# Transposing the keys once and copying them to the other partitions, and moving three steps in the order of a hybrid attention, Hyena and MoE layer

## The chip, the cores and the metric

One core of one Trainium2 chip runs the whole kernel. The metric is the device time of one execution in microseconds (us); of several executions the median is taken. The engines are TensorE (PE, with its weight loads as PEld), VectorE (DVE), ScalarE (ACT), GpSimd (POOL) and SyncE (SP), which here only issues DMAs.

## The reference

The layer serves 1024 latent tokens and 128 context tokens with the same weights. The part that the change touches, cut down:

```python
h = x * (1 + sc1) + sh1                       # modulation columns, from SiLU(cond) @ w_mod
proj = h @ w_in                               # "in-projection": q, k, v and three Hyena parts
q, k = rope_2d(rms_norm(q)), rope_2d(rms_norm(k))
k_all = concatenate([k, cached context keys]) # 2 kv heads of 64, 8 query heads
s = einsum(q, k_all) * scale ; p = softmax(s) ; o = p @ v_all

z = position_features(t)                      # Hyena's filters
h = sin(freq * (z @ w1 + b1))                 # first sine layer
h = sin(freq * (h @ w2 + b2))                 # second sine layer
h = (h @ w3) * exp(-t * |decay|)              # the taps, in a window
g = two_sided(h) ; g = g * rsqrt(sum(g * g))  # norm of each channel
spec = rfft(g)                                # spectra of the filters
```

After that come two gated long convolutions by Fourier transforms, the output projection, a layer norm, a router, 33 blocks of experts and a last layer norm.

## The kernel before

Each engine has its own list of instructions, written out by hand and run in that order. Engines wait for each other on named counting semaphores (`pe.wait_ge(sem("skip_scaled"), n)`). So what stands behind a waiting instruction on the same engine waits too.

**Front.** PE multiplies the conditioning vectors with eight 1 MB chunks of `w_mod`: `modulation_parts(c)` is the product (16 records on L1139), ACT's `copy_parts(c)` brings it to SBUF, and `modulation_columns(c)` sums it into columns. Chunks come by DMA on SP's queue in order; chunks 4 to 7 are issued when an earlier product is done. Between them stand `hidden(0)` and `hidden(1)`, the two products of the sine layers. DVE turns each product into an argument (L1853 to L1858) and ACT takes the sine (L846).

**Four passes.** The filters are made in four passes of 256 channels. In pass p, `taps(p, j)` on PE makes nine tiles of taps, DVE weighs them (`weigh_taps`), ACT squares them (L863), and POOL adds the squares (L650, L654, L648). `norms(p)` on PE sums these over partitions (four products with one column); DVE makes scales of them (`norm_scales`) and releases `skip_scaled`; `skip_rows(p)` on PE turns the scales into rows, which DVE adds to the first row of taps (L1626 on 1x512 elements) before it releases `taps_skipped`. DVE also makes the tiles of the transform, in three parts that release `tiles_transformed`. `spectrum(p, i)` on PE makes 22 products per pass, each copied by ACT (L871) and stored by a DMA. In between stand the 27 tiles of the in-projection, `project_qkv(m)`: eight products of 128x256 each, copied by ACT (L879). Tiles 0 to 2 are in pass 0's first part, and pass p starts with tile `first` = 5, 12 or 19. The first tiles need the modulated input, which ACT makes in `modulate` (L903, eight instructions for the first 512 tokens). The last five spectra of a pass are left over into the next one (`SPEC_LEFT`).

**Keys.** Before attention, keys and queries are split into a high and a low part (`split_keys`, `high_heads`, `low_heads` on DVE), turned by PE, and copied from PSUM by ACT. The contraction of a score runs over 128 partitions: a query's high part in 0 to 63 and its low part in 64 to 127, against a key part that stands in both halves. `KEY_BLOCKS` are four blocks (2 kv heads, high and low) of ten tiles of 128 keys. `turn_keys(n)` makes both halves by two ordinary products with the identity per tile (L1374, `tile_position` 0 and 64), and ACT copies 128x1280 (L995). Then `scores(0)` starts the attention loop of 72 steps (9 query tiles, 8 heads), in which DVE takes the maximum (L2056), ACT the exponent (L1004), and PE turns the probabilities (L1113) and multiplies them with the values (L1443).

Of the kernel before, what the change touches and what calls it, by code (L numbers as in the profile page):

```python
# [22 lines left out]
F32 = mybir.dt.float32  # L23
# [133 lines left out]
def build(nc, I, O):  # L157
    ctx = ExitStack()
    with ctx:
# [17 lines left out]
        def sem(name):  # L177
            if name not in sems:
                sems[name] = ctx.enter_context(nc.semaphore(name))
            return sems[name]  # L180
# [638 lines left out]
        def _(act):  # L819
# [172 lines left out]

            for n, (v, s) in enumerate(KEY_BLOCKS):
                act.wait_ge(sem("rows_turned"), n + 1 + (n > 1))
                act.copy(kT[:, s, v, :], PS[:, 1536 * (n % 2):1536 * (n % 2) + 10 * P]).then_inc(sem("rows_copied"), 1)  # L995
                if n == 1:
                    act.wait_ge(sem("rows_turned"), 3)
                    act.copy(qT[:, :, 0:P], PS[:, 3072:4096].rearrange("p (h t) -> p h t", h=HEADS)).then_inc(sem("rows_copied"), 1)
# [109 lines left out]
        def _(pe):  # L1108
# [17 lines left out]
            def modulation_parts(c):  # L1126
                if c < COND_CHUNKS:
                    pe.wait_ge(sem(f"cond_w_loaded{c % 4}"), 16 * (c // 4 + 1))
                else:
                    pe.wait_ge(sem("late_w_loaded"), 16 * (c - COND_CHUNKS + 1))  # L1130
                if c > COND_CHUNKS:
                    pe.wait_ge(sem("mod_copied"), c - COND_CHUNKS)
                if c:
                    pe.wait_ge(sem("parts_copied"), c)
                at = 512 * parts_bank(c)
                for half in range(2):
                    for j in range(4):
                        k = 2 * j + half
                        last = nc.tensor.matmul(PS[32 * j:32 * j + 32, at:at + CHUNK], cond_wide[:, k, :], mod_weights(c)[:, k, :],  # L1139
                                                start=half == 0, stop=half == 1, tile_position=(0, 32 * j))  # L1140
                last.then_inc(sem("parts_product"), 1)

            def modulation_columns(c):
                pe.wait_ge(sem("parts_copied"), c + 1)
                for i in range(2):
                    last = mm(bank(7, 2, at=2 * (2 * c + i)), parts(c)[:, P * i:P * (i + 1)], part_sum)
                last.then_inc(sem("cols_product"), 1)
# [29 lines left out]
            def skip_rows(p):  # L1177
                pe.wait_ge(sem("skip_scaled"), p + 1)
                for lc in range(2):
                    for b in range(2):  # L1180
                        last = mm(bank(4 + lc, P, rows=1, at=HALF + P * b), col_s[:, 2 * b + lc:2 * b + lc + 1], ident)
                last.then_inc(sem("skip_row"), 1)
# [37 lines left out]
            modulation_parts(0)  # L1220
            modulation_parts(1)
            modulation_columns(0)
            modulation_parts(2)
            modulation_columns(1)
            hidden(1)
            for c in range(3, 6):
                modulation_parts(c)
                modulation_columns(c - 1)
# [15 lines left out]
            for p in range(PASSES):  # L1244
                first, end = QKV_BY_PASS[p:p + 2]
                if p:
                    project_qkv(first)
                    for i in range(SPEC_LEFT, N_SPEC):
                        spectrum(p - 1, i)
                    norms(p)  # L1250
                    project_qkv(first + 1)
                    project_qkv(first + 2)
                    skip_rows(p)
                    project_qkv(first + 3)
                    project_qkv(first + 4)
                else:
                    norms(0)
                    skip_rows(0)
                    for m in range(3):
                        project_qkv(m)  # L1260
                for i in range(SPEC_CTX):
                    spectrum(p, i)
                for m in range(first + (5 if p else 3), end):
                    project_qkv(m)
                for i in range(SPEC_CTX, SPEC_ODD):
                    spectrum(p, i)
                for i in range(SPEC_ODD, SPEC_LEFT):
                    spectrum(p, i)
                if p + 1 == PASSES:
                    for i in range(SPEC_LEFT, N_SPEC):  # L1270
                        spectrum(p, i)
                    continue
                for j in range(NTILE):
                    taps(p + 1, j)
# [90 lines left out]
            def turn_keys(n):  # L1365
                v, s = KEY_BLOCKS[n]
                pe.wait_ge(sem("rows_split"), n + 1 + (n > 1))
                if n >= 2:
                    pe.wait_ge(sem("rows_copied"), n - 1)
                for t in range(NTILE + 1):  # L1370
                    key = {NLAT: 9, NTILE: 8}.get(t, t)
                    at = 1536 * (n % 2) + P * key
                    for u in range(2):
                        last = nc.tensor.matmul(PS[HD * u:HD * (u + 1), at:at + P], k_split[:, s, t, HD * v:HD * (v + 1)].bitcast(F32),  # L1374
                                                ident, start=True, stop=True, tile_position=(0, HD * u))
                last.then_inc(sem("rows_turned"), 1)

            def turn_head(out, h):
# [19 lines left out]
            def scores(i):  # L1398
                h, t = ATT[i]
                v = h // GQA  # L1400
                pieces = ((0, 512), (512, 1024), (1024, 1152)) if t < NLAT else ((1152, 1280),)
                if i:
                    pe.wait_ge(sem("max_ready"), i)
                if t and h == 0:
                    pe.wait_ge(sem("heads_copied"), 4 * t)
                for s in range(2):
                    for a, (k0, k1) in enumerate(pieces):
                        last = mm(bank(a, k1 - k0), qT[:, h, P * t:P * (t + 1)], kT[:, s, v, k0:k1], s == 0, s == 1)
                last.then_inc(sem("scores_ready"), 1)

            def turn_probs(i):
                n = NTILE if ATT[i][1] < NLAT else 1
                if i:
                    pe.wait_ge(sem("probsT_d"), i)
                if i - 1 in HEADS_AT:
                    pe.wait_ge(sem("heads_copied"), 4 * HEADS_AT[i - 1][0] + HEADS_AT[i - 1][1] // 2 - 3)
                if i in HEADS_AT:
                    turn_heads(i)
                pe.wait_ge(sem("exp_ready"), i + 1)
                if i:  # L1420
                    pe.wait_ge(sem("probsT_a"), i)
                for k in range(n):
                    last = turn(PS[:, 1536 + P * k:1536 + P * (k + 1)], probs[:, i % 2, P * k:P * (k + 1)])
                last.then_inc(sem("probs_transposed"), 1)
# [37 lines left out]
                last.then_inc(sem("scales_spread"), 1)  # L1462

            pe.wait_ge(sem("rows_copied"), len(KEY_BLOCKS) + 1)
            scores(0)
            for i in range(len(ATT)):
                if i + 1 < len(ATT):
# [140 lines left out]
        def _(dve):  # L1608
# [434 lines left out]
                tt(q_split[:, :, 1, :], q, q_split[:, :, 0, :].bitcast(F32), ALU.subtract).then_inc(sem("rows_split"), 1)  # L2043

            dve.wait_ge(sem("cache_loaded"), 32)
            split_keys(0)
            high_heads(0)
            low_heads(0)
            split_keys(1)

            def maximum(i):
                n = NTILE * P if ATT[i][1] < NLAT else P
# [12 lines left out]
            for i in range(len(ATT)):  # L2065
                if i + 1 < len(ATT):
                    maximum(i + 1)
                dve.wait_ge(sem("probs_transposed"), i + 1)
                if i >= 4:
                    dve.wait_ge(sem("attn_product"), i // 2 - 1)  # L2070
                if ATT[i][1] < NLAT:
                    dve.tensor_copy(probsT[:, i % 4, 4:9, :], PS[:, 2048:2688].rearrange("p (t n) -> p t n", t=5)).then_inc(  # L2072
                        sem("probsT_d"), 1)
                else:
                    give(dve.tensor_copy(bn[:, 0:1], ones[:, 0:1]), "probsT_d")
                if i in HEADS_AT:
                    t, h = HEADS_AT[i]
                    dve.tensor_copy(qT[:, h:h + 2, P * t:P * (t + 1)],
                                    bank(5, 2 * P, at=P).rearrange("p (h t) -> p h t", h=2)).then_inc(sem("heads_copied"), 1)
                h, t = ATT[i]  # L2080
                if t + 1 < NTILE and h == 0:
                    dve.wait_ge(sem("rows_turned"), 5 + t if t else 3)
                    high_heads(t + 1)
                    low_heads(t + 1)
                if i in SCALE_AT:
                    scale_attention(SCALE_AT[i])
# [264 lines left out]
```

## Time and profile before

| | |
|---|---|
| median of 3 runs | 1656.86 us (1655.42 to 1658.33) |
| the profiled execution's own time | 1657.55 us |
| its span in the trace | 1655.7 us |
| PE busy | 1501.1 us (91%) |
| DVE, ACT, POOL busy | 947.7, 362.8, 367.4 us |
| filters and in-projection | 0 to 300 us, PE busy 253.9 |
| keys turned, first scores | 726.3 to 740.4 us |

Times in the rows count from the span's start. A row of a timeline gives start, length, engine, line, operation and count, and in brackets how long the engine sat idle before it and who released it. A product of f32 operands leaves two records, a transpose one. The share of busy time says little here, since PE is busy nearly everywhere: a change can only act where PE sits idle, or runs at its lower clock, or is given less work.

### The profile page before, as it was taken

To read this page: it belongs to the slowest core of one execution; us is meant where nothing else is said; L and a number is where in the kernel's file an instruction comes from. 1 tells how busy PE (TensorE), PEld (TensorE's weight loads), DVE (VectorE), ACT (ScalarE), POOL (GpSimd) and SP (SyncE) were. 2 spreads that over 40 slices of the span, in tenths; PEclk is the share of its full clock that TensorE was granted. 3 is DMA by queue.
4 is the path that set the end of the run, shared out by engine and by line. 5 is a ranking of instruction groups with operands and counts; after the bars stand their busy time and mean duration, and the time that the engine had idled before them with its cause. 6 is when DMAs were issued, how large, how long until landed. Compare 5 with 4: busy or idle time off the path is not lost. (4 is left out here: it accounts for less than half of the span.)

```text
span 1655.7 us, 22893 instructions
## 1 busy us (share of the span) xinstructions
PE 1501.1 (91%) x8630; PEld 1086.7 (66%) x8630; DVE 947.7 (57%) x1577; ACT 362.8 (22%) x696; POOL 367.4 (22%) x623
## 2 busy tenths in 40 slices
PE   7689988999998899949999997999489999999985
PEld 3467766444444688848888874455378888888852
DVE  3867876366654999966666653443733333333326
ACT  2553342111110111115655551010000000000004
POOL 0330330011110000000311317746222212222114
PEclk9799998999999999979999997999589999999998
DMA  9422123233321212230000004211458898998845
GB/s 320 148 69 83 44 75 118 67 104 122 122 90 67 90 58 64 70 109 1 2 2 1 2 1 155 74 64 51 165 202 319 338 331 321 332 338 327 306 171 218
DMA packets 102743, 229.27 MB, mean 138 GB/s; under 512 B 12807, under 2 KB 70759, under 8 KB 93896
## 3 DMA queue, kind: packets, MB, share of 16 engines
q1 hardware_dynamic: 78968, 195.86, 33.1%
q0 software_dynamic: 10736, 19.77, 3.4%
q10 hardware_dynamic: 12960, 12.59, 2.3%
q8 instruction: 50, 0.82, 0.2%
q14 instruction: 29, 0.24, 0.0%
HBM read 204.66 MB, written 38.98 MB: 147 GB/s over the span
## 5 line engine op out<-in xcount | busy, mean ns | idle before, releaser
L1110 PE MATMUL PS<-buffer 128*128 128x128 f32 (+7 forms) x5638 | 1255.5, 380 | 90.6 <-DVE buffer L1626 28.1
L1110 PEld LDWEIGHTS PS<-buffer 128*128 128x128 f32 (+2 forms) x5638 | 870.6, 195 | 448.0 <-issue 314.1
L1626 DVE TENSOR_TENSOR buffer<-buffer 128x512 f32<-128x512 f32 (+16 forms) x446 | 258.5, 604 | 26.8 <-ACT buffer L965 11.8
L1626 DVE TENSOR_TENSOR buffer<-PS,buffer 128x512 f32<-128x512 f32 (+2 forms) x143 | 94.4, 690 | 129.6 <-PE PS L1110 116.2
L1113 PE MATMUL PS<-buffer 128*128 128x128 f32 x1136 | 157.0, 280 | 12.7 <-DMA buffer<-moe_inputs,buffer 5.5
L1113 PEld LDWEIGHTS PS<-buffer 128*128 128x128 f32 x1136 | 130.2, 153 | 39.9 <-issue 29.0
L1626 DVE TENSOR_TENSOR buffer<-buffer,PS 128x256 f32<-128x256 f32 (+3 forms) x55 | 27.6, 502 | 205.7 <-PE PS L1110 195.1
L2056 DVE TENSOR_SCALAR_CACHE_REDUCE buffer<-PS 128x1152 f32<-128x1152 f32 (+1 forms) x72 | 89.1, 1238 | 36.4 <-PE PS L1110 35.6
L1004 ACT ACTIVATE buffer<-buffer 128x1152 f32<-128x1152 f32 (+1 forms) x72 | 83.8, 1164 | 107.6 <-DVE buffer L2056 107.5
L1080 ACT ACTIVATE buffer<-PS 128x256 f32<-128x256 f32 x33 | 12.6, 383 | 367.1 <-PE PS L1110 367.1
L2072 DVE COPY buffer<-PS 128x640 f32<-128x640 f32 x64 | 52.8, 825 | 63.1 <-PE PS L1113 62.3
L1443 PE MATMUL PS<-buffer 128*64 128x128 f32 x1168 | 79.3, 279 | 6.1 <-ACT buffer L1037 4.7
L1443 PEld LDWEIGHTS PS<-buffer 128*64 128x64 f32 x1168 | 62.6, 137 | 19.7 <-ACT buffer L1037 13.8
L678 POOL TENSOR_TENSOR buffer<-buffer 128x256 f32<-128x256 f32 (+4 forms) x45 | 17.9, 399 | 258.1 <-ACT buffer L1010 254.7
L1966 DVE TENSOR_SCALAR buffer<-PS,buffer 128x1024 f32<-128x1024 f32 (+1 forms) x24 | 21.0, 877 | 93.8 <-PE PS L1110 93.4
L2257 DVE SCALAR_TENSOR_TENSOR buffer<-PS,buffer 128x1024 f32<-128x1024 f32 x33 | 42.4, 1284 | 40.5 <-PE PS L1110 40.5
L662 POOL TENSOR_TENSOR buffer<-buffer 2x256 f32<-2x256 f32 x16 | 11.9, 746 | 235.4 <-ACT buffer L841 235.4
L1639 DVE SCALAR_TENSOR_TENSOR buffer<-buffer 128x512 f32<-128x512 f32 (+6 forms) x69 | 56.6, 820 | 2.4
L770 POOL COPY buffer<-buffer 128x1 int32 x32 | 5.8, 183 | 232.4 <-DVE buffer L2257 232.4
L2241 DVE COPY buffer<-PS 128x1024 f32<-128x1024 f32 x33 | 40.4, 1225 | 17.6 <-PE PS L1113 17.6
L648 POOL TENSOR_TENSOR buffer<-buffer 128x256 f32<-128x256 f32 x8 | 8.7, 1085 | 168.2 <-ACT buffer L863 168.2
L761 POOL DMA_INDIRECT expert_outputs<-buffer x34 | 34.4, 1012 | 47.1 <-POOL buffer L770 25.5
(170 smaller groups left out, 966.2 us busy)
## 6 DMA issues: line engine op xcount, KB each, us to landing
buffer<-in_exp_w_gate SPq DMA_DIRECT2D x33, 1024.0 KB, 6.8
buffer<-in_exp_w_up SPq DMA_DIRECT2D x33, 1024.0 KB, 9.2
buffer<-in_exp_w_down SPq DMA_DIRECT2D x33, 1024.0 KB, 9.0
buffer<-in_w_mod SPq DMA_DIRECT2D x24, 1024.0 KB, 7.0
filter_spectra<-buffer ACTq DMA_DIRECT2D x88, 128.0 KB, 1.7
buffer<-filter_spectra SPq DMA_DIRECT2D x44, 256.0 KB, 2.6
buffer<-in_w_in SPq DMA_DIRECT2D x9, 1024.0 KB, 5.2
buffer<-expert_outputs SPq DMA_DIRECT2D x4, 1536.0 KB, 17.1
```

Of the source, the lines that this page charges most:

```text
L761: pool.indirect_dma_start(out=y_d[:, :], out_offset=bass.IndirectOffsetOnAxis(ap=rows, axis=0), in_=ybuf[:, s, :], in_offset=None, bounds_ ...
L1004: act.activation(probs[:, i % 2, 0:n], probs[:, i % 2, 0:n], ACT.Exp, bias=nmax[:, i:i + 1], scale=-1.0, accum_out=psums[:, i:i + 1]).then ...
L1110: return nc.tensor.matmul(out, lhsT, rhs, start=start, stop=stop)
L1113: return nc.tensor.transpose(out, in_, ident)
L1443: last = nc.tensor.matmul(PS[HD * u:HD * (u + 1), at:at + P], vals, probsT[:, (first + u) % 4, a, :], start=a == 0, stop=a == len(tiles) - ...
L1626: return dve.tensor_tensor(out, a, b, op)
L1639: own(dve.scalar_tensor_tensor(out, a, s, b, ALU.mult, op))
L1966: own(dve.tensor_scalar(out[:, t0:t1], PS[:, ps0 + t0:ps0 + t1], w[1], w[3], ALU.mult, ALU.add))
L2056: dve.tensor_scalar(probs[:, i % 2, 0:n], PS[:, 0:n], -1.0, None, ALU.mult, ALU.min, accum_out=nmax[:, i:i + 1]).then_inc(sem("max_ready"), 1)
L2072: dve.tensor_copy(probsT[:, i % 4, 4:9, :], PS[:, 2048:2688].rearrange("p (t n) -> p t n", t=5)).then_inc(sem("probsT_d"), 1)
L2241: dve.tensor_copy(xgT[:, s, :, :], PS[:, 0:1024].rearrange("p (k n) -> p k n", k=KT)).then_inc(sem("xT_ready"), 1)
L2257: dve.scalar_tensor_tensor(ybuf[:, s, :], PS[:, 2048:3072], row_scale[:, s, 0:1], row_gain, ALU.mult, ALU.mult).then_inc(sem("y_ready_to_s ...
```

## The change

Three edits.

1. `turn_keys` makes one transpose per tile, into partitions 0 to 63. ACT copies 64x1280 instead of 128x1280. A new step on DVE, `double_keys(n)`, copies each block from partitions 0 to 63 to 64 to 127, ahead of the first maximum. PE waits for it before `scores(0)`. The semaphore of the query copies is merged with that of the key copies; their waits count four higher.
2. `hidden(1)` stands before `modulation_parts(2)` instead of behind `modulation_columns(1)`.
3. In pass 0, in-projection tiles 0 and 1 stand between `norms(0)` and `skip_rows(0)`. In passes 1 to 3 one tile moves ahead of `norms(p)`, and the others close up.

```diff
@@ ACT
-                act.copy(kT[:, s, v, :], PS[:, 1536 * (n % 2):1536 * (n % 2) + 10 * P]).then_inc(sem("rows_copied"), 1)
+                act.copy(kT[0:HD, s, v, :], PS[0:HD, 1536 * (n % 2):1536 * (n % 2) + 10 * P]).then_inc(sem("rows_copied"), 1)
@@ PE
             modulation_columns(0)
+            hidden(1)
             modulation_parts(2)
             modulation_columns(1)
-            hidden(1)
@@ PE
+                    project_qkv(first + 1)
                     norms(p)
-                    project_qkv(first + 1)
                     project_qkv(first + 2)
+                    project_qkv(first + 3)
                     skip_rows(p)
-                    project_qkv(first + 3)
                     project_qkv(first + 4)
                 else:
                     norms(0)
+                    project_qkv(0)
+                    project_qkv(1)
                     skip_rows(0)
-                    for m in range(3):
-                        project_qkv(m)
+                    project_qkv(2)
@@ PE
-                    for u in range(2):
-                        last = nc.tensor.matmul(PS[HD * u:HD * (u + 1), at:at + P], k_split[:, s, t, HD * v:HD * (v + 1)].bitcast(F32),
-                                                ident, start=True, stop=True, tile_position=(0, HD * u))
+                    last = turn(PS[0:HD, at:at + P], k_split[:, s, t, HD * v:HD * (v + 1)].bitcast(F32))
@@ PE
             pe.wait_ge(sem("rows_copied"), len(KEY_BLOCKS) + 1)
+            pe.wait_ge(sem("scores_side_copied"), len(KEY_BLOCKS))
             scores(0)
@@ DVE
+            def double_keys(n):
+                v, s = KEY_BLOCKS[n]
+                dve.wait_ge(sem("rows_copied"), n + 1 + (n > 1))
+                dve.tensor_copy(kT[HD:P, s, v, :], kT[0:HD, s, v, :].bitcast(F32)).then_inc(sem("scores_side_copied"), 1)
+
             split_keys(0)
             high_heads(0)
             low_heads(0)
             split_keys(1)
+            for n in range(len(KEY_BLOCKS)):
+                double_keys(n)
```

PE's list in passes 0 and 1 of the kernel before, from the last taps of pass 0 on. `128x1 x4` is `norms`, `1x128 x4` is `skip_rows`, `128x512` are taps, and `128x256` are in-projection tiles (eight each) and spectra.

```order
L1110 MATMUL PS<-buffer 128x512 x4
L1110 MATMUL PS<-buffer 128x1 x4
L1110 MATMUL PS<-buffer 1x128 x4
L1110 MATMUL PS<-buffer 128x256 x66
L1110 MATMUL PS<-buffer 128x512 x9
L1110 MATMUL PS<-buffer 128x256 x18
L1110 MATMUL PS<-buffer 128x1 x4
L1110 MATMUL PS<-buffer 128x256 x16
```

The same place with the change.

```order
L1110 MATMUL PS<-buffer 128x512 x4
L1110 MATMUL PS<-buffer 128x1 x4
L1110 MATMUL PS<-buffer 128x256 x16
L1110 MATMUL PS<-buffer 1x128 x4
L1110 MATMUL PS<-buffer 128x256 x50
L1110 MATMUL PS<-buffer 128x512 x9
L1110 MATMUL PS<-buffer 128x256 x26
L1110 MATMUL PS<-buffer 128x1 x4
L1110 MATMUL PS<-buffer 128x256 x16
```

In pass 0 two tiles (16 products) moved from behind the skip rows to ahead of them; in pass 1 one tile moved ahead of the norms (26 products there instead of 18).

PE's list from the last products of the convolutions to the first scores, before. `L1374` are the keys, `L1113` the eight query heads.

```order
L1110 MATMUL PS<-buffer 128x256 x352
L1374 MATMUL PS<-buffer 64x128 x40
L1113 MATMUL PS<-buffer 128x128 x8
L1374 MATMUL PS<-buffer 64x128 x40
L1110 MATMUL PS<-buffer 128x512 x2
```

The same place with the change.

```order
L1110 MATMUL PS<-buffer 128x256 x352
L1113 MATMUL PS<-buffer 64x128 x20
L1113 MATMUL PS<-buffer 128x128 x8
L1113 MATMUL PS<-buffer 64x128 x20
L1110 MATMUL PS<-buffer 128x512 x2
```

The number of instructions for the keys is halved, and they are transposes now.

DVE's list from the last split of the keys to the first maxima, as a piece of the difference.

```order
 L1626 TENSOR_TENSOR buffer<-buffer 128x9x64
 L1626 TENSOR_TENSOR buffer<-buffer 128x64
-L2056 TENSOR_SCALAR buffer<-PS 128x1152 x2
-L2072 COPY buffer<-PS 128x640
+L2049 CAST buffer<-buffer 64x1280 x4
+L2063 TENSOR_SCALAR buffer<-PS 128x1152 x2
+L2079 COPY buffer<-PS 128x640
```

Four copies of 64x1280 are new, ahead of the maxima, whose lines are only renumbered.

## Rows read from the trace of the kernel before

**Rows 1.** The page, busy time of PE: us, share, instructions.

```profile
PE 1501.1 (91%) x8630; PEld 1086.7 (66%) x8630; DVE 947.7 (57%) x1577; ACT 362.8 (22%) x696; POOL 367.4 (22%) x623
```

**Rows 2.** Timeline of PE, 5 to 82 us.

```profile
18.95 1.94 PE L1139 MATMUL PS<-buffer 128*32 128x256 f32 x16 [3.04 <-DMA buffer<-in_w_mod]
20.81 5.04 PE L1110 MATMUL PS<-buffer 128*128 128x2 f32 x10
...
41.76 1.07 PE L1139 MATMUL PS<-buffer 128*32 128x256 f32 x16
...
65.20 14.56 PE L1110 MATMUL PS<-buffer 128*1 128x128 f32 x60 [5.44 <-DVE buffer L1626]
81.12 1.26 PE L1110 MATMUL PS<-buffer 128*128 128x256 f32 x3 [1.36 <-ACT buffer L871]
```

**Rows 3.** Timeline of ACT, 0 to 75 us.

```profile
16.67 1.16 ACT L846 ACTIVATE buffer<-buffer 64x1152 f32<-64x1152 f32 x1 [1.27 <-DVE buffer L1858]
...
54.98 0.63 ACT L863 ACTIVATE buffer<-buffer 128x512 f32<-128x512 f32 x1 [3.76 <-POOL buffer L654]
55.51 5.74 ACT L903 ACTIVATE buffer<-buffer 128x512 f32<-128x512 f32 x8
72.02 0.37 ACT L879 COPY buffer<-PS 128x256 f32<-128x256 f32 x1 [10.77 <-PE PS L1110]
```

**Rows 4.** Timeline of DVE, 0 to 75 us.

```profile
25.97 1.47 DVE L1853 TENSOR_SCALAR buffer<-PS,buffer 64x1152 f32<-64x1152 f32 x1 [9.33 <-PE PS L1110]
...
31.81 0.75 DVE L1858 TENSOR_SCALAR buffer<-buffer 64x1152 f32<-64x1152 f32 x1
...
64.78 0.36 DVE L1626 TENSOR_TENSOR buffer<-buffer 128x4 f32<-128x4 f32 x2
```

**Rows 5.** Timeline of SP's queue: the issue of chunk 7 of `w_mod`.

```profile
27.78 0.55 SPq L468 DMA_DIRECT2D buffer<-in_w_mod  x1
```

**Rows 6.** DMA issues, 27.5 to 28.4 us: count, KB, us to landing.

```profile
buffer<-in_w_mod SPq DMA_DIRECT2D x1, 1024.0 KB, 13.4
```

**Rows 7.** Windows: us, busy of PE, PEld, DVE, ACT, POOL, granted clock, DMA.

```profile
65.20:69.60 4.40, 4.40 (x14) 3.01 (x15) 4.20 (x7) 0.00 (x0) 0.00 (x0) 0.50 0.01 4
...
704.50:707.88 3.38, 1.68 (x6) 0.96 (x6) 3.38 (x9) 0.59 (x1) 0.00 (x0) 1.00 0.00 0
...
726.27:731.70 5.43, 5.43 (x52) 5.43 (x54) 3.26 (x8) 0.85 (x1) 0.00 (x0) 0.50 0.90 253
...
738.60:742.00 3.40, 1.83 (x16) 1.20 (x12) 0.21 (x1) 1.23 (x1) 0.00 (x0) 1.00 0.23 95
742.00:749.00 7.00, 4.95 (x30) 3.88 (x30) 5.50 (x9) 3.17 (x5) 0.00 (x0) 1.00 0.01 4
```

**Rows 8.** Timeline of DVE, pass 1.

```profile
124.96 0.16 DVE L1886 TENSOR_SCALAR buffer<-PS 128x4 f32<-128x4 f32 x1 [0.72 <-PE PS L1110]
...
134.66 1.39 DVE L1626 TENSOR_TENSOR buffer<-buffer,PS 1x512 f32<-1x512 f32 x2
```

**Rows 9.** Timeline of ACT, pass 1, and the last copy of keys.

```profile
139.97 0.37 ACT L879 COPY buffer<-PS 128x256 f32<-128x256 f32 x1 [3.08 <-PE PS L1110]
140.40 0.37 ACT L871 COPY buffer<-PS 128x256 f32<-128x256 f32 x1
...
739.12 1.23 ACT L995 CAST buffer<-PS 128x1280 fp32r<-128x1280 f32 x1 [0.96 <-PE PS L1374]
```

**Rows 10.** Timeline of PE, 700 to 760 us.

```profile
726.27 7.26 PE L1374 MATMUL PS<-buffer 128*64 128x128 f32 x80 [16.85 <-DVEq L2033]
...
740.39 1.36 PE L1110 MATMUL PS<-buffer 128*128 128x512 f32 x6 [1.32 <-ACT buffer L995]
743.21 1.37 PE L1110 MATMUL PS<-buffer 128*128 128x512 f32 x6 [1.46 <-DVE buffer L2056]
744.60 1.20 PE L1113 MATMUL PS<-buffer 128*128 128x128 f32 x9
...
752.21 1.42 PE L1113 MATMUL PS<-buffer 128*128 128x128 f32 x11
```

More of the change, by code:

```diff
@@ L1404, in scores @@
                 if t and h == 0:
-                    pe.wait_ge(sem("heads_copied"), 4 * t)
+                    pe.wait_ge(sem("scores_side_copied"), 4 * t + 4)
                 for s in range(2):
@@ L1415, in turn_probs @@
                 if i - 1 in HEADS_AT:
-                    pe.wait_ge(sem("heads_copied"), 4 * HEADS_AT[i - 1][0] + HEADS_AT[i - 1][1] // 2 - 3)
+                    pe.wait_ge(sem("scores_side_copied"), 4 * HEADS_AT[i - 1][0] + HEADS_AT[i - 1][1] // 2 + 1)
                 if i in HEADS_AT:
@@ L2078, in _ @@
                     dve.tensor_copy(qT[:, h:h + 2, P * t:P * (t + 1)],
-                                    bank(5, 2 * P, at=P).rearrange("p (h t) -> p h t", h=2)).then_inc(sem("heads_copied"), 1)
+                                    bank(5, 2 * P, at=P).rearrange("p (h t) -> p h t", h=2)).then_inc(sem("scores_side_copied"), 1)
                 h, t = ATT[i]
```

## The prediction

> **What bounds the kernel now.** I read the page first: PE is busy for 1501.1 us, 91% of the span [rows 1], so a change can gain only where PE idles, runs at its lower clock, or loses work. The timeline of PE then shows the idle places that the edits touch. PE stands still for 5.44 us ahead of 65.20, where DVE releases the skip rows [rows 2]. ACT had the first half of the modulated input ready at 55.51 + 5.74 = 61.25 [rows 3], so tiles 0 and 1 of the in-projection could have run from there. At the keys PE starts at 726.27, and the first scores start at 740.39 [rows 10], 14.12 us later. Last I read the granted clock by windows: it was 1.2 GHz from 65.20 to 69.60 and from 726.27 to 731.70 [rows 7], so both places begin at half speed.
>
> **Edit 2, the second sine layer first.** `hidden(1)` needs the first sine, done at 16.67 + 1.16 = 17.83 [rows 3]. PE was idle until 18.95, waiting for chunk 2; the product is most of the 5.04 us at 20.81 (I take 4.0 of them; the rest are four records of columns) [rows 2]. So it runs 17.9 to 21.9, `modulation_parts(2)` slips by 3.0 us to 21.9, and from chunk 3 on PE is 0.9 us ahead, having filled that much of its idle time. DVE starts its argument at 22.0 instead of 25.97 [rows 4]. This earliness meets a load: chunk 7 is issued at 27.78 and takes 13.4 us to land [rows 5, 6], so 41.18, and its product ran at 41.76 [rows 2]. In the code `modulation_parts(7)` stands ahead of taps 4 to 8, and `copy_parts(7)` ahead of ACT's third square; nothing behind them can come more than 0.55 us sooner. The issue of chunk 6 waits for the product that slips, but 13.4 us to landing is a queue with many microseconds of other loads in it, so a slip of 3 us is covered; if it were not, up to 2 us would be lost. Behind the third square stands POOL's chain of sums, which releases ACT's last one at 54.98 [rows 3], and behind that `modulate`. Edit 2: **0.5 us**, between -1 and 1.
>
> **Edit 3, pass 0.** Tile 0 then starts at 61.25 - 0.5 = 60.75, where PE's work started at 65.20: the same work, from a start 4.45 us earlier (edit 2's 0.5 is in it). The clock rose 4.4 us after PE restarted here, and 5.4 us after at the keys [rows 7]; with 5.4, one more microsecond at half speed costs 0.5. The skip rows fall behind tile 1, about 71 instead of 67. DVE needs them at 71.91 - 0.5 for the row sums; until 65.14 it makes the scales [rows 4], and then tiles of the transform. The two meet within some tenths. The wait of 1.36 us at 81.12, for ACT to copy a spectrum behind the second half of `modulate` [rows 2], moves along with tile 2. So edits 2 and 3 bring 4.45 - 0.5, about **4.0 us**, by the first tap of pass 1; bounds 2.4 and 5.6, for a low stretch that is 3 us longer or shorter, at half speed.
>
> **Edit 3, passes 1 to 3.** Norms come one tile later, and tiles follow each other in 0.37 + 3.08 = 3.45 us [rows 9]. DVE waited 0.72 us for them in pass 1 [rows 8], so it is 3.45 us late there; for passes 2 and 3 I take the same as a bound. Who waits for DVE? `taps_skipped` came at 134.66 + 1.39 = 136.05 [rows 8] and comes at 139.5. The first spectrum behind it ran right behind the tile that ACT copied at 139.97, and was itself copied at 140.40 [rows 9], so with 0.6 us from start to copy it started near 139.8. That leaves 0.3 us: hidden, barely. PE has no idle time to fill ahead of these norms, so nothing is gained either: **0**, three times.
>
 The copy on DVE is new: 0.75 us for 64x1152 from SBUF [rows 4] scales to 0.83 for 1280; the bound above is the rate from PSUM, 1.47 for 1152 [rows 4], so 1.63. The first three hide behind copies of ACT; only the fourth shows. Scores start 10.85 us after PE's start, for 14.12: **3.3 us** earlier (2.0 to 4.4, by DVE's copy and the rise of the clock).
>
> **What it may give back.** PE now does less just ahead of the loop: from the last turn at 8.4 it idles for 2.4 us, does `scores(0)` (1.36), and idles 1.46 for the first maximum, as before [rows 10]. From 704.50 to 707.88 PE worked 1.68 us, and the clock was low after it; from 738.60 to 742.00 it worked 1.83 us and the clock stayed [rows 7]. In the changed kernel the like stretch holds about 1.4 us of work. So I expect the clock to fall to 1.2 GHz around the second scores, and to rise when PE is dense again. Some 6 us at half speed (5.4 at the keys [rows 7]) cost 3.0, less what PE's short waits absorb: **2.6 us** lost, bounds 1 and 4.
>
> **A rule that speaks against edit 1.** From 742 to 749 us a third of PE's work is transposes (1.20 us per step beside 1.4 of scores [rows 10]), PE works 4.95 of 7 us, and the clock stays up [rows 7]: here they seem to count as work, which gives the 3.3. The Trainium skill (TensorE: Matmul & The Clock Gate, Part 4: PE-mode transpose) says that a transpose does not count as PE-busy in the same way. By that rule the rise would not come during the turns, which is rival B.
>
> **The sum.** 4.0 + 3.3 - 2.6 = 4.7 us. From the profiled execution's own 1657.55 that is 1652.85; this execution stands 0.7 above the median of the runs, and I take the sum from the median, 1656.86: **1652.2 us**.
>
> **Rivals.** A measurement of this kernel tells about 0.2%, 3.3 us, from no change.
> - *Forecast, 45%*: 1652.2, its own range 1650 to 1654.5.
> - *A, the clock does not fall in the loop's start, 27%*: 4.0 + 3.3 = 7.3, so 1649.6. For it: at 738.6 it held with little work. Against it: PE will do less still.
> - *B, the clock does not rise on transposes, 8%*: all 48 turns at 0.22 us are 10.6, scores start at 12.9 and gain 1.2 only. The loop then runs at half speed until products alone keep PE dense, an estimated 20 us, 10 lost: 10 - 4.0 - 1.2 = 4.8 slower, 1661.7. For it there is no row in which the clock rose on transposes; against it, 742 to 749.
> - *C, the late norms reach PE, 7%*. DVE is 3.45 us late in each of passes 1 to 3. With 0.3 us of room it is hidden; without any it is 10.35 us, 1656.86 - 4.7 + 10.35 = 1662.5, slower. It decides from about 1.6 us of lateness per pass. For it: 0.3 us is little. Against it: between the norms and `taps_skipped` DVE waits for nothing but the skip rows, and PE's tiles in between are the same number as before.
> - *D, the start in pass 0 is not used, 13%*: the change doesn't do there what it says, because ACT is late or the clock stays low longer; 1 us instead of 4.0, so 1655.2.
>
> **How the numbers follow.** Range 1647.0 to 1657.5: down to A with a clock that falls less often elsewhere, up past D and a weak C; B, most of C and a little below A lie outside. *Faster by over 0.2%* (below 1653.6): 0.38 of the forecast's 0.45, all of A, a little of D, 0.67. *Slower* (above 1660.2): most of B and C, 0.11. *Same*: 0.22.
>
> **What the next profile would show.** Right: DVE's second L1853 near 22.0; tile 0 near 60.7 and its copy by ACT near 67 instead of 72.02; the wait at 81.12 near 77; the first norm scale of pass 1 behind some 4 us of idle DVE, and no wait of PE for DVE at the spectra; the first scores 10.5 to 11.5 us after the first turn; new DVE copies of 0.8 us; a stretch at 1.2 GHz early in the loop. Wrong: PE waiting for DVE in passes 1 to 3, DVE copies above 1.2 us, a low clock through all turns, tile 0 not before 63. What would spoil the number with every step right is the clock: it was low in other stretches too, and each microsecond more or less of that is half a microsecond of time.

## The result and the profile after

The changed kernel takes 1647.17 us, the median of 5 runs (1644.95 to 1649.25); before, on the same chip, it was 1656.86 (1655.01 to 1658.33). The ratio is 0.994, with a 95% interval of 0.9924 to 0.9956: 9.9 us faster by the ratio, 9.7 by the medians, where 4.7 was forecast. On two more chips the same kernel stood at 0.9936 (0.9915 to 0.9958) and 0.9950 (0.9932 to 0.9969). The time lies in the stated range, and the larger chance (0.67, faster by over 0.2%) was on what came; the sum was half of the gain. The profiled execution took 1644.95 for 1657.55, 12.6 us less, so this pair of profiles shows more than the medians do. All ratios compare ordinary executions alone; only e5 below had two others among its 12 (2587 and 7635 us).

First the page of the changed kernel, busy time (answers to [rows 1]). PE has 120 instructions fewer and is busy 6.2 us less, half of what was gained; the rest was idle time.

```profile
PE 1494.9 (91%) x8510; PEld 1080.9 (66%) x8510; DVE 954.3 (58%) x1581; ACT 362.6 (22%) x696; POOL 368.6 (22%) x623
```

The timeline of PE, 15 to 90 us (answers to [rows 2]): start, length, engine, line, number of records, and in brackets the idle time ahead and who ended it.

```profile
17.97 4.10 PE L1110 MATMUL PS<-buffer 64*64 64x512 f32 x6 [0.60 <-ACT buffer L846]
...
41.60 1.07 PE L1139 MATMUL PS<-buffer 128*32 128x256 f32 x16 [1.46 <-DMA buffer<-in_w_mod]
...
58.86 15.94 PE L1110 MATMUL PS<-buffer 128*128 128x1 f32 x68 [8.88 <-POOL buffer L648]
76.16 14.00 PE L1110 MATMUL PS<-buffer 128*128 128x256 f32 x62 [1.36 <-ACT buffer L871]
```

`hidden(1)` stands at 17.97, PE then meets chunk 7 of `w_mod`, and the 5.44 us of idle time behind the norms are gone: the eight records of the norms and 60 more run in one piece. The timeline of ACT, 52 to 80 us, answers to [rows 3]:

```profile
53.81 0.63 ACT L863 ACTIVATE buffer<-buffer 128x512 f32<-128x512 f32 x1 [2.25 <-POOL buffer L654]
54.35 5.74 ACT L903 ACTIVATE buffer<-buffer 128x512 f32<-128x512 f32 x8
65.91 0.37 ACT L879 COPY buffer<-PS 128x256 f32<-128x256 f32 x1 [5.82 <-PE PS L1110]
```

`modulate` starts 1.16 us earlier (54.35 for 55.51), and tile 0 is copied 6.11 earlier, since the skip rows no longer stand ahead of it. By the wait of 1.36, at 76.16 for 81.12, 4.96 us are left. In this profile tile 0 stood behind the norms and not behind `modulate`, which was done at 60.09; in ten of the twelve profiles with the pass 0 edit PE waits 1.64 us for `modulate` there, as the forecast had it. The clock was low for 3.2 us of tile 0, where it was low for 4.4 behind PE's restart before (windows of the changed kernel, columns as in [rows 7]):

```profile
60.56:63.80 3.24, 3.24 (x9) 2.61 (x10) 2.93 (x10) 0.00 (x0) 0.00 (x0) 0.50 0.03 8
63.80:67.00 3.20, 3.20 (x16) 2.81 (x15) 2.89 (x10) 1.09 (x3) 0.00 (x0) 1.00 0.00 0
```

In pass 1 the profile gains 2.9 more, and that is the clock's. The windows of before and then of the changed kernel from 116 to 124 us:

```profile
116.00:124.00 8.00, 5.64 (x15) 4.60 (x15) 6.49 (x5) 2.43 (x7) 3.77 (x4) 0.59 0.19 66
```

```profile
116.00:124.00 8.00, 8.00 (x43) 7.15 (x42) 6.16 (x18) 0.75 (x2) 0.00 (x0) 1.00 0.12 41
```

Pass 2 gave 1.4 of it back. Of all profiled executions, 7 of the 11 with both the sine and the pass 0 edit lack this low stretch, and 2 of the 9 without both: scatter for a good part, and no step of the prediction.

The keys, on the timeline of PE (answers to [rows 10]), on that of DVE, and by windows:

```profile
717.44 7.92 PE L1113 MATMUL PS<-buffer 128*64 128x128 f32 x48 [16.60 <-DVEq L2033]
727.64 1.33 PE L1110 MATMUL PS<-buffer 128*128 128x512 f32 x6 [2.29 <-DVE buffer L2049]
730.43 2.40 PE L1110 MATMUL PS<-buffer 128*128 128x512 f32 x6 [1.46 <-DVE buffer L2063]
732.62 2.12 PE L1113 MATMUL PS<-buffer 128*128 128x128 f32 x9
734.40 2.20 PE L1110 MATMUL PS<-buffer 128*128 128x512 f32 x6
736.43 1.15 PE L1113 MATMUL PS<-buffer 128*128 128x128 f32 x9
```

```profile
725.55 0.82 DVE L2049 CAST buffer<-buffer 64x1280 fp32r<-64x1280 f32 x1 [1.55 <-ACT buffer L995]
726.67 0.82 DVE L2049 CAST buffer<-buffer 64x1280 fp32r<-64x1280 f32 x1 [0.30 <-ACT buffer L995]
```

```profile
717.44:722.60 5.16, 5.16 (x25) 4.49 (x26) 4.08 (x9) 1.89 (x2) 0.00 (x0) 0.50 0.84 251
722.60:729.40 6.80, 4.08 (x31) 3.46 (x29) 2.86 (x4) 3.90 (x4) 0.00 (x0) 1.00 1.02 406
729.40:736.20 6.80, 5.77 (x20) 5.10 (x21) 3.72 (x7) 3.17 (x5) 0.00 (x0) 0.50 0.16 65
982.00:1002.50 20.50, 12.09 (x66) 8.61 (x66) 3.72 (x16) 5.23 (x19) 14.04 (x42) 0.50 0.76 292
```

From the first turn to the first scores it is 10.20 us for 14.12. The clock rose at 722.6, while PE had done nothing but turns since 717.44, and fell again at 729.4: the second scores took 2.40 us for 1.37. Behind the loop (last row) the clock was low for 20.5 us; before, for 23.9:

```profile
994.60:1018.50 23.90, 14.62 (x66) 9.90 (x67) 7.83 (x20) 4.61 (x14) 18.21 (x42) 0.50 0.74 265
```

Comparing start times of the same instruction in the two traces, the 12.6 us of this pair come so: edit 2, 1.2; pass 0, 3.8; clock in passes 1 and 2, 1.5; the end of pass 3, 2.6; turns and copies of the keys, 3.9; low clock early in the loop, -1.7; low clock behind the loop, 2.8. That is 14.1; small losses between (0.3 ahead of the keys, 0.5 in the loop, 0.7 behind it) make it 12.6. Three of these places the prediction did not have: the clock in passes 1 and 2, the end of pass 3, and the clock behind the loop.

One pair of profiles holds much scatter. The experiments below left 18 more, and the averages over the profiles with an edit, less those without it, come nearer to the 9.9 of the runs: start of `modulate` 1.5 (edit 2), from there to the wait of 1.36 3.6 (pass 0), end of pass 3 1.4, keys 3.9, the low clock early in the loop with what comes back behind it -0.6. The sum is 9.8.

### The profile page after: what moved, and what is told of

Same layout as the page of the kernel before. It is cut to its first block, busy times and chain, and to the rows that moved or that the text cites. A ratio compares the mean times of both kernels' runs of the same rounds, so it can differ in the third digit from the quotient of the medians.

```text
span 1643.1 us, 22658 instructions
## 1 busy us (share of the span) xinstructions
PE 1494.9 (91%) x8510; PEld 1080.9 (66%) x8510; DVE 954.3 (58%) x1581; ACT 362.6 (22%) x696; POOL 368.6 (22%) x623
## 4 chain that ended last, share of the span: by engine, by line
PE 76%; DVE 8%; DMA 5%; POOL 4%; issue 4%; ACT 2%; SPq 0%; ACTq 0%; DVEq 0%; POOLq 0%
PE PS L1110 63%; PE PS L1113 7%; PE PS L1442 4%; DVE buffer L1626 3%; DMA buffer<-in_w_mod 3%; PE PS L1139 2%; POOL buffer L654 1%; POOL buffer L650 1%; DVE buffer L1728 1%; DMA buffer<-expert_outputs 1%; DVE buffer L2063 1%; PE PS L1459 1%; ACT buffer L871 1%; DMA filter_spectra<-buffer 0%; ACT buffer L1037 0%
## 5 line engine op out<-in xcount | busy, mean ns | idle before, releaser
L1110 PE MATMUL PS<-buffer 128*128 128x128 f32 (+6 forms) x5638 | 1253.9, 380 | 85.1 <-DVE buffer L1626 22.7
L1113 PE MATMUL PS<-buffer 128*128 128x128 f32 (+1 forms) x1176 | 164.3, 284 | 29.2 <-DVEq L2033 16.6
L1113 PEld LDWEIGHTS PS<-buffer 128*128 128x128 f32 (+1 forms) x1176 | 136.9, 154 | 57.4 <-issue 28.2
L1626 DVE TENSOR_TENSOR buffer<-buffer,PS 128x256 f32<-128x256 f32 (+3 forms) x55 | 27.5, 501 | 206.6 <-PE PS L1110 196.0
L1442 PEld LDWEIGHTS PS<-buffer 128*64 128x64 f32 x1168 | 62.7, 137 | 19.4 <-ACT buffer L1037 13.6
```

The lines of the kernel that those rows point to most:

```text
L1110: return nc.tensor.matmul(out, lhsT, rhs, start=start, stop=stop)
L1113: return nc.tensor.transpose(out, in_, ident)
L1626: return dve.tensor_tensor(out, a, b, op)
```

## The experiments

### Each edit alone

E1 is the change's edit of the keys alone, e2 the sine layer, e3 the order in pass 0, e4 the order in passes 1 to 3, each the diff's own lines put into the kernel before.

> Edit 1 alone on the kernel before: one transpose per key tile, ACT's copy of 64 partitions, DVE's copy to the other 64. Theory M (each edit is worth what its own place shows): first scores 10.2 us after the first turn instead of 14.1, then a stretch at 1.2 GHz that gives 1.7 back; 2.2 us faster, 1654.7, between 1653 and 1656. Theory S (the surplus of the whole change sits in this edit, in the attention loop or behind it): 4 us or more faster. Theory L (the surplus is how the clock's low stretches happened to fall): as M for the median, with a spread of about 1.5 us.

> Edit 2 alone: the second sine layer ahead of the third modulation product. Theory M: the modulated input is ready 0.5 to 1.2 us sooner, and the skip rows on PE too; 0.5 to 1.2 us faster, 1656. Theory S (the surplus comes from this edit's earlier DVE work): 2 us or more faster, and PE's start in pass 0 (65.20 before) earlier by as much. Theory L: as M.

> Edit 3 in pass 0 alone: tiles 0 and 1 between the norms and the skip rows of pass 0. Theory M: tile 0 starts at 61.3 instead of behind the skip rows at 65.2; 3.5 to 4.2 us faster, 1653.0. Theory S (surplus in pass 0 itself): 5 us or more by the first taps of pass 1. Theory L: 4 at the first taps of pass 1, what comes behind it differs by the clock alone.

> Edit 3 in passes 1 to 3 alone: one in-projection tile moved ahead of the norms in each. Theory M and L: within 0.5 us of the kernel before in the median, 1656.9; DVE's first scale of pass 1 behind about 4 us of idle time; PE waits for no DVE result at the spectra. Theory S (the later norms themselves help, so that PE or ACT saves time in passes 1 to 3): 2 to 3 us faster, with the time saved between 118 and 300 us. The rival of the late norms: 1 us or more slower.

Against the kernel before, on one chip (10 to 12 runs each):

```
            median    ratio    95% interval       gain by the ratio
e1 keys     1654.44   0.9982   0.9972 to 0.9992   3.0
e2 sine     1655.14   0.9993   0.9982 to 1.0004   1.2
e3 pass 0   1653.21   0.9972   0.9959 to 0.9984   4.6
e4 1 to 3   1655.67   0.9991   0.9981 to 1.0002   1.5
```

The four add up to 10.3, the whole change to 9.9: they don't help or hinder each other by more than can be told. The prediction had 4.0 for e2 and e3 together (measured 5.8), 0 for e4 (1.5) and 3.3 - 2.6 = 0.7 for e1 (3.0). All three terms are too small, and none of the misses alone explains the difference. Only the first is clear of noise: e1's interval, 1.3 to 4.6 us, leaves 0.7 out, while the other two intervals reach down to the forecast.

### The end of pass 3

Where did e4 gain? Its tiles run as before up to 257 us. Then, on SyncE's queue, before and e4:

```profile
273.98 0.33 SPq L468 DMA_DIRECT2D buffer<-in_rot  x1
```

```profile
277.06 0.33 SPq L468 DMA_DIRECT2D buffer<-in_rot  x1
```

SyncE waits for `tiles_transformed` to reach 3 * PASSES and then issues three loads of 512, 1024 and 1024 KB. VectorE is a tile later, so they are 3.1 us later. The timeline of ACT in the kernel before shows what they meet, stores of spectra that ACT's next copies wait for; then e4's:

```profile
277.51 0.37 ACT L871 COPY buffer<-PS 128x256 f32<-128x256 f32 x1 [1.86 <-DMA filter_spectra<-buffer]
...
281.30 0.37 ACT L871 COPY buffer<-PS 128x256 f32<-128x256 f32 x1 [3.41 <-DMA filter_spectra<-buffer]
```

```profile
283.21 0.37 ACT L871 COPY buffer<-PS 128x256 f32<-128x256 f32 x1 [4.04 <-DMA filter_spectra<-buffer]
284.94 0.37 ACT L871 COPY buffer<-PS 128x256 f32<-128x256 f32 x1 [1.36 <-DMA filter_spectra<-buffer]
```

The long waits begin 3.5 us later and the first of them ends 5.7 us later, with four more spectra through; the last one is copied 2.5 us earlier. About 1.5 us of this is idle time of PE (5.2 to 3.75 us), the rest the clock, low for 6.8 us there instead of 10.2. So a late VectorE was a gain. How large varies: from the copy of the last in-projection tile to that of the last spectrum, the eight profiles with the old order and the loads not held take 23.4 us on average (21.2 to 24.5), six with the new one 22.0 (21.3 to 23.1), so 1.4 us, where this pair shows 2.6. To test that it is the loads, e5 (before) and e6 (changed) hold them until the fourth product from the end, e10 (before) and e9 (changed) until all stores but the last three are through:

```
 sp.wait_ge(sem("tiles_transformed"), 3 * PASSES)
+sp.wait_ge(sem("spectrum_product"), PASSES * N_SPEC - 4)                 # e5, e6
+for r in range(3): sp.wait_ge(rs["spec"][r], SPEC_STORED[r] - 16)        # e9, e10
 load(rot, I["rot"], "gains_loaded")
```

> The kernel before, with the three loads that SyncE issues behind the last transform of the filters (rotary tables, a chunk of w_in, a chunk of w_mod) held back until the fourth spectrum from the end of pass 3 is made; no order of norms or skip rows is changed. Theory M (these loads delay the stores of the spectra, so that ScalarE's copies and then TensorE wait): ScalarE's waits for stores of 1.86, 3.41 and 1.85 us from 277.51 on are gone or below 0.7 us each, the last spectrum is copied 2.5 to 5 us sooner, and the time is 2 to 4 us below before. Rival theory R (what the run with later norms in passes 1 to 3 gained at the end of pass 3 was the clock's, not the loads'): the waits shrink or not, but the time stays within 1 us of before, or is longer because the held loads are late for the first products that need them.

> The changed kernel with the same hold on the three loads. Theory M: ScalarE's waits for stores at the end of pass 3 (2.25, 2.75 and 1.84 us in the changed kernel's profile) go, TensorE's idle 1.95 + 1.18 us there with them, so 2 to 3 us below the changed kernel, about 1644.5. Rival R: 1647, as the changed kernel.

> The changed kernel with the three loads behind the last transform held back until all spectra but the last three are stored, so that no copy of ScalarE can wait for a store that shares the DMA engines with them. Theory M (the loads delay the stores): ScalarE's waits for stores and TensorE's 5.03 us of idle time ahead of the first feature product (profile of the run with the shorter hold) are both gone; 7.1 of them is in the feature products already in the changed kernel, so the gain over it is at the last spectrum 3 us, kept to the end unless the w_mod chunk is late for its product (302 us before): 1643 to 1645 where the changed kernel takes 1647 to 1649. Rival R: no change, or slower by the late loads.

> The kernel before with the same hold. Theory M: TensorE's idle time of 1.06 + 3.12 + 1.03 us at the end of pass 3 goes, and the end of that stage is 4 to 6 us earlier than before, with no idle 5 us behind it as the shorter hold had; time 3.5 to 5.5 us below before. Rival R: within 1 us of before.

E5 came to 1656.91, ratio 0.9989 (0.9979 to 1.0): 1.8 us, a little under what was expected and not clear of zero. E6 came to 1650.88, 0.9961 (0.9947 to 0.9975): 6.5 us, some 3 less than the changed kernel gained, against theory M's number. PE, in e6, shows why: the short waits are gone and a long one stands in their place, for the last stores, which now meet the loads.

```profile
276.51 5.42 PE L1111 MATMUL PS<-buffer 128*128 128x256 f32 x24 [0.16 <-ACT buffer L872]
286.95 9.40 PE L1111 MATMUL PS<-buffer 128*128 128x512 f32 x16 [5.03 <-ACT buffer L872]
```

E10 came to 1653.89, 0.9982 (0.9972 to 0.9993): 3.0 us, clear of zero but under the 3.5 to 5.5 expected; its PE waits 2.07 us for the `w_mod` chunk, as e9's does. E9 came to 1645.52, 0.9929 (0.9909 to 0.9948), as the changed kernel on that chip (e12, 0.9936). Its profile is 6.0 us ahead of the changed kernel's at the last spectrum, with no wait for a store (15.6 us from the last tile's copy to the last spectrum's, in e9, e10 and e13 alike, with the clock never low there); then the `w_mod` chunk, third in the queue, is late, and later low stretches of the clock take the rest:

```profile
279.63 7.13 PE L1112 MATMUL PS<-buffer 128*128 128x512 f32 x16 [0.72 <-ACT buffer L873]
289.05 1.94 PE L1141 MATMUL PS<-buffer 128*32 128x256 f32 x16 [2.29 <-DMA buffer<-in_w_mod]
```

So e13 holds the loads as e9 does and issues the chunk that is needed first before the other two (`load_w_mod(COND_CHUNKS)` ahead of `load(rot, ...)`).

> The changed kernel with the three loads held back until all spectra but the last three are stored, and the w_mod chunk issued first, then the rotary tables and the w_in chunk. Theory M (the loads' place is worth time): no wait for stores at the end of pass 3, and TensorE's wait of 2.29 us for in_w_mod, seen with the same hold in the old order of the loads, goes as well: 2 to 4 us below the changed kernel. Rival: these waits go, but the clock stays low longer in the stages behind and takes it back, as it did with the first hold (same time as the changed kernel).

1642.15 us, ratio 0.9917 (0.9897 to 0.9936), 13.8 us below before, and 5.5 by the ratios, 6.1 by the medians, below the changed kernel on the same chip (e16), more than the 2 to 4 expected: the fastest version of this study. Against the mean of the changed kernel's three ratios (0.9942) it is 4.1 us. PE waits neither for the stores nor for the chunk:

```profile
282.74 7.13 PE L1112 MATMUL PS<-buffer 128*128 128x512 f32 x16 [0.70 <-ACT buffer L873]
289.80 1.07 PE L1141 MATMUL PS<-buffer 128*32 128x256 f32 x16
```

### Leaving the edit of passes 1 to 3 out, and the yardsticks

E7 and e14 are the changed kernel with the old order in passes 1 to 3, e12 and e16 the changed kernel again.

> The changed kernel with the old order of norms and skip rows in passes 1 to 3 (the changed kernel less that one edit). Theory M: VectorE finishes the last transform some 3 us sooner, the loads collide with the spectra's stores earlier, and the end of pass 3 is 1.5 to 2.5 us longer: about 1649. By the prediction, which put this edit at 0: 1647.2, as the changed kernel.

> The changed kernel unchanged (one empty line more), on the same chip as the other three, as their yardstick: 9.7 us below before if the first measurement stands, and by the sum of the four single edits (3.0 + 1.2 + 4.6 + 1.5 = 10.3) between 9 and 11.

> The changed kernel with the old order of norms and skip rows in passes 1 to 3, a second time, beside the changed kernel on the same chip. If the edit is worth what it gained alone: 1.5 us above the changed kernel. If it is worth what the prediction said: the same time within 0.7.

> The changed kernel once more, as the yardstick for the other three on this chip: 9 to 11 us below before.

E7: 1648.96, 0.9943 (0.9928 to 0.9959). E14: 1649.61, 0.9957 (0.9942 to 0.9972), beside e16 on one chip, 1648.26, 0.9950 (0.9932 to 0.9969). E12: 1645.45, 0.9936. The mean of the changed kernel's three ratios is 0.9942, of these two 0.9950: 1.3 us, close to e4's 1.5, but each of the intervals is wider than that. The edit is worth between nothing and 3 us; the mechanism is shown by the profiles, its size in the time is not settled. E14's own profile warns how much one profile can say: with the old order it is as short at the end of pass 3 (21.2 us) as the changed kernel's (21.6).

### How much room the norms had

E15 puts `norms(p)` behind `project_qkv(first + 2)`, one tile later than the change does.

> The changed kernel with the norms of passes 1 to 3 one in-projection tile later still, behind first + 2, so VectorE is another 3.45 us late. The prediction counted 0.3 us of room ahead of the first spectrum behind taps_skipped. If that count is right and the changed kernel had used it up: TensorE waits for VectorE about 3.1 us in each of three passes and the time is 8 to 9.5 us above the changed kernel. If there was more room than counted (the changed kernel showed no such wait): less than 3.1 per pass, down to the changed kernel's time.

1667.79 us, 1.0050 (1.0026 to 1.0073): slower than before, and 19.5 us above the changed kernel (e16). PE waits for VectorE in each pass, where the changed kernel's row of the same place has no such wait (e15 first, the changed kernel second):

```profile
134.85 15.36 PE L1110 MATMUL PS<-buffer 128*128 128x256 f32 x62 [3.07 <-DVE buffer L1626]
```

```profile
133.91 15.71 PE L1110 MATMUL PS<-buffer 128*128 128x256 f32 x70 [0.15 <-ACT buffer L871]
```

3.07 us, three times, for the 3.1 expected: the count of the room was right, and the change used all of it. The time is twice as far off as the 8 to 9.5 us expected. Three waits are 9.2 us, and the profiled execution took 1654.81, 9.9 above the changed kernel's profiled one. But only 3 of the 10 runs lay there; 7 lay near 1668, 13 us higher. What those have more of is open, as none of them was profiled.

### The low clock early in the loop

E8 fills PE's idle time with products that nobody reads, e11 with turns (on the changed kernel); e18 does e11's on edit 1 alone, and e17 is edit 1 alone again.

```
 turn_keys(3)
+pe.wait_ge(sem("rows_copied"), 3)
+filler(18)                             # e11, e18: turn(PS[:, 3072:3200], ident); e8: 10 of mm(bank(6, 512), ident, qkv[:, 0, 0:512])
 ...
 pe.wait_ge(sem("scores_side_copied"), len(KEY_BLOCKS))
 scores(0)
+filler(12)                             # e8: 6
```

> The changed kernel with 10 products of ident by 128x512 added behind the last key turn and 6 between the first and the second scores, whose results nobody reads; they fill TensorE's idle 2.29 and 1.46 us. If the low clock from 729.4 on comes from the idle time ahead of it: no low stretch there, scores(1) in 1.36 us instead of 2.40, and 1 to 1.7 us below the changed kernel, if the filling itself delays the scores by less than 0.3 us. Rival: the stretch is there whatever TensorE does in these gaps, and the time is the changed kernel's or up to 1 us more.

> The changed kernel with 18 turns of ident (0.11 us each, 2.0 us) behind the last key turn and 12 (1.3 us) between the first and the second scores. The earlier filling took two instructions of 0.43 us for each product, 13.8 us in all instead of 3.8, and so delayed the loop by 6.9; these fit the gaps. If the low clock from 729.4 on comes from the idle time ahead of it: no low stretch early in the loop, second scores in 1.36 us, 1.5 to 2.5 us below the changed kernel. Rival: low stretch as in the changed kernel, time the same or up to 0.5 us more.

> Edit 1 alone, a second time: 3.0 us below before as the first time; low stretch early in the loop, low stretch behind the loop 20.5 us long.

> Edit 1 alone with 18 turns of ident behind the last key turn and 12 between the first and the second scores, which keep the clock high early in the loop. If the low clock there costs what the prediction took (2.6) or what the changed kernel's profile shows at the place (1.7): 1.5 to 2.5 us below the run of edit 1 alone. If it is given back behind the loop (low stretch there 23.9 us instead of 20.5, 2.8 us): the same time within 1, or slightly above.

E8 was badly sized: each product became two instructions of 0.43 us, 13.8 us in place of 3.75, and the loop started 6.9 us late; 1656.67, 0.9994 (0.9983 to 1.0005). No low stretch was there all the same. E11 shows that the gaps are the cause; all eleven profiles with edit 1 and no filling have the low stretch, the three with filling have none. The timeline of its PE, 712 to 755 us:

```profile
721.97 10.20 PE L1113 MATMUL PS<-buffer 128*64 128x128 f32 x66 [17.54 <-DVEq L2041]
732.49 1.34 PE L1110 MATMUL PS<-buffer 128*128 128x512 f32 x6 [0.32 <-DVE buffer L2057]
733.67 1.48 PE L1113 MATMUL PS<-buffer 128*128 128x128 f32 x12
735.29 1.37 PE L1110 MATMUL PS<-buffer 128*128 128x512 f32 x6
```

The second scores take 1.37 us for 2.40. From the first turn to the fourth scores this profile wins 3.6 us on the kernel before, the changed kernel's 2.2. Yet the time is 1646.68, 0.9935 (0.9918 to 0.9953), that of e12. On edit 1 alone, e18 is 1655.24, 0.9979 (0.9966 to 0.9992) beside e17's 1655.86, 0.9983 (0.9971 to 0.9994): 0.6 us by either figure, where 1.5 to 2.5 was the expectation if the stretch cost its price. Both comparisons scatter by more than 2 us, so the times alone don't decide. Where it goes is seen in part in the profiles: of the 11 profiles with the low stretch early in the loop, 7 have 20.5 us of low clock behind the loop, as the changed kernel has, and 2.8 us come back there (two have 23.9, two 27.3); all 9 profiles without it, three of them filled, have 23.9. From the fourth scores to the end of that stretch the eleven win 1.3 us on average and the nine 0.2. So this low clock costs 1.7 us where it stands and, on average, 0.6 in the end. Why the two are tied is open.

## Why the prediction was wrong, step by step

The mechanisms of the edits were those of the forecast; the sum was half of the result, because most of one term that it took off is not lost, one zero is not zero, and two terms were too small.

- **"What it may give back: 2.6 us lost" is the step that failed.** The clock fell where it was forecast (729.4, around the second scores) and rose when PE was dense, but cost 1.7 at the place, of which some 1.1 came back behind the loop, and filling the gaps brought nothing on the changed kernel and 0.6 on edit 1 alone. The term should have been about 0.6: edit 1 alone gained 3.0 and 2.8 (e1, e17), where the forecast left it 0.7. Rival A's time (1649.6) is nearest of all, but by luck: its condition, no fall of the clock, is not what happened.
- **"Edit 3, passes 1 to 3: 0" failed too, by about 1.4** in the profiles, though the times alone would allow nothing to 3. VectorE was late by a tile and hidden, as argued: DVE's wait for the norms, 0.72 [rows 8], became 4.08 us in e4, for some 4 forecast, with no PE wait, and e15 confirmed the 0.3 us of room. The step asked who waits for DVE among the engines and left out SyncE, whose three loads hang on the last `tiles_transformed` at the end of pass 3, a place of which the prediction shows no row. In the changed kernel's profile it is 1.29, since PE, without the low stretch of pass 1, reached the norms sooner (the two rows stand below this list).
- **Edits 2 and 3 in pass 0: 4.0, measured 5.8 (e2 and e3) and 4.96 in the profile, inside the bounds 2.4 to 5.6 there.** Pass 0 alone was 3.8 for 3.5. Edit 2 was 1.2 for 0.5. The forecast held chunk 7's landing for fixed and so allowed 0.55 at most. PE met the load at 41.60 as forecast, within 0.16 of its place before; what lies behind that and still came a microsecond sooner in this profile is POOL's chain. But the place itself varies by microseconds from one profile to the next, and the profile before was a lucky one: of the eight without edit 2 it has the earliest start of `modulate` (55.5, the others 56.0 to 60.0, mean 57.0), while the twelve with edit 2 have 54.3 to 57.5, mean 55.5. That is 1.5 us for edit 2, give or take 1.2; e2's own interval reaches from 0.7 lost to 3.0 gained.
- **Edit 1: 3.3, measured 3.9 at the place.** DVE's copy was 0.82 for 0.83 and only the fourth showed; the turns took 7.92 for 8.7, because the clock rose 5.2 us after the first one with 25 done, and the later ones ran at 0.11. From the first turn to the first scores the eleven profiles with edit 1 and no filling take 9.8 us on average (9.3 to 10.2), six without it 13.6 (13.3 to 14.1): 3.9 again.
- **The rule against edit 1** (the Trainium skill, TensorE: Matmul & The Clock Gate, Part 4: PE-mode transpose: a transpose does not count as PE-busy in the same way) is not borne out here: the clock rose at 722.6 with nothing but turns behind it since 717.44, and e11's turns, in the gaps around the first scores, kept it high. So rival B did not happen.
- **Rival C did not happen, and was one tile away** (e15). **Rival D did not happen**: tile 0 was copied at 65.91, for 67 forecast.

DVE's wait for the norms of pass 1, e4 and then the changed kernel:

```profile
128.62 0.16 DVE L1886 TENSOR_SCALAR buffer<-PS 128x4 f32<-128x4 f32 x1 [4.08 <-PE PS L1110]
```

```profile
120.58 0.16 DVE L1886 TENSOR_SCALAR buffer<-PS 128x4 f32<-128x4 f32 x1 [1.29 <-PE PS L1110]
```

By the ratios of the single edits: 2.3 too little for the keys, 1.8 for the sine and pass 0, 1.5 for passes 1 to 3, 5.6 in all, where the whole is 5.0 to 5.2 off. By the averages over profiles: 2.0 for what was not lost, 1.4 for passes 1 to 3, 1.0 for edit 2, 0.6 for edit 1 and 0.1 for pass 0, 5.1 in all.

## What to carry to other kernels

When a step makes an engine late, ask also which queues wait for it: a DMA issued later can be worth more than the wait that was feared, and holding bulk loads behind small stores that a copy waits for, with the load that is needed first at their head, brought as much here (4 to 5.5 us, e13) as the forecast had for the whole change. Do not book a low stretch of the clock at its full price: what it costs on the spot and what filling it returns in the time are two measurements. An order that hides a delay exactly leaves no room: one more tile cost 10 to 20 us. And a single profile is one draw: the pair here showed 12.6 us and the runs 9.9, and the forecast took as a fixed limit a load whose landing moved by microseconds between profiles.

## What was not expected of the hardware

ACT waited 3.41 us (before) and 4.04 us (e4) for stores of 128 KB, which land in 1.7 us in the median (e13), once 2.5 MB of loads had been issued. Turns alone took the clock from 1.2 to 2.4 GHz, 3.1 to 5.2 us after the first turn in the eleven profiles. On POOL, additions of 128x256 that take 0.73 us took 2.24 and 2.12 while DVE worked on 128x1536 (2.02 and 2.16 us) beside them; that the one slows the other is not tested here:

```profile
50.45 2.24 POOL L650 TENSOR_TENSOR buffer<-buffer 128x256 f32<-128x256 f32 x1
52.77 2.12 POOL L654 TENSOR_TENSOR buffer<-buffer 128x256 f32<-128x256 f32 x1
54.85 0.72 POOL L650 TENSOR_TENSOR buffer<-buffer 128x256 f32<-128x256 f32 x1
```

These are of the kernel before; both stand ahead of the square at 54.98 [rows 3], and in the changed kernel's profile only one does.
